# Reordering one of seven Strassen-Winograd products, and the vector work beside it, in the feed-forward stages of a two-layer streaming encoder

## What is computed

```python
def swiglu(h, w_in, w_out):
    gu = h @ w_in
    gate, up = gu[..., :D_FF], gu[..., D_FF:]
    return (jax.nn.silu(gate) * up) @ w_out
# twice per layer: h_res + 0.5 * swiglu(rms_norm(h_res, g), w_in, w_out)
```

## Time and profile before

| | |
|---|---|
| median of 3 runs | 2357.1 us |
| the profiled execution | 2354.26 us |
| its span, first to last instruction | 2352.5 us |
| TensorE matmul busy | 2325.6 us (99%) |
| TensorE weight load busy | 2214.3 us (94%) |
| VectorE busy | 1678.2 us (71%) |
| ScalarE busy | 1242.6 us (53%) |
| granted TensorE clock, mean | 1.0 of full speed |

### The profile page before, as it was taken

The page is one execution under the profiler, slowest core; times in us unless marked ns, Lnnn a source line. Parts: engine busy times, 40 slices in busy tenths (PEclk is TensorE's granted clock), DMA queues, the critical chain, the costliest instruction groups (busy, mean ns, idle before and its releaser), DMA issues.

```text
span 2352.5 us, 43321 instructions
## 1 busy us (share of the span) xinstructions
PE 2325.6 (99%) x17809; PEld 2214.3 (94%) x17809; DVE 1678.2 (71%) x2748; ACT 1242.6 (53%) x2011; POOL 346.3 (15%) x454
## 2 busy tenths in 40 slices
PE   7999999999999999999999999999999999999999
PEld 7999999999999999999999999999888777998997
DVE  8855854899895488568778558548999855874773
ACT  8734733454455477356567347344544455762751
POOL 1101101112212211011011011011222122110110
PEclk9999999999999999999999999999999999999999
DMA  6845736676768968458458457366776698773753
GB/s 179 183 121 144 173 88 154 146 154 149 155 138 199 209 137 182 117 141 187 113 141 182 119 146 168 87 154 149 157 158 150 141 225 190 158 187 102 169 134 110
DMA packets 111365, 358.71 MB, mean 152 GB/s; under 512 B 12608, under 2 KB 12608, under 8 KB 111168
## 3 DMA queue, kind: packets, MB, share of 16 engines
q0 software_dynamic: 64080, 210.53, 44.0%
q1 hardware_dynamic: 46720, 145.08, 21.1%
q10 hardware_dynamic: 368, 0.33, 0.0%
HBM read 351.41 MB, written 2.10 MB: 150 GB/s over the span
## 4 chain that ended last, share of the span: by engine, by line
PE 89%; DVE 5%; ACT 2%; DMA 2%; issue 1%; POOL 0%; DVEq 0%; ACTq 0%
PE po L1102 28%; PE po L1119 23%; PE po L1170 21%; PE ptr L1119 7%; PE pov L1119 5%; DVE cv L1757 1%; DMA wla<-in_mixes 1%; PE pov L1349 1%; PE pov L1352 1%; PE pstat L1309 1%; DMA wha<-in_mixes 1%; PE ptr L1318 1%; PE pov L1289 0%; PE pstat L1274 0%; DVE wlb L1518 0%
## 5 line engine op out<-in xcount | busy, mean ns | idle before, releaser
L1102 PE MATMUL po<-xh,wha 128*128 128x264 f32 (+1 forms) x1408 | 345.5, 312 | 2.7 <-DMA wla<-in_mixes 2.0
L1102 PE MATMUL po<-xl,wha 128*128 128x264 f32 (+1 forms) x1408 | 335.5, 305 | 0.0
L1102 PE MATMUL po<-xh,wla 128*128 128x264 f32 (+1 forms) x1408 | 334.8, 304 | 0.0
L1757 DVE SCALAR_TENSOR_TENSOR cv<-ub,lp,cv 128x528 f32<-128x528 f32 (+1 forms) x480 | 333.3, 753 | 1.7
L1170 PE MATMUL po<-hh,wla 128*128 128x264 f32 (+1 forms) x1232 | 283.7, 300 | 0.0
L1170 PE MATMUL po<-hl,wha 128*128 128x264 f32 (+1 forms) x1232 | 283.7, 300 | 0.0
L1170 PE MATMUL po<-hh,wha 128*128 128x264 f32 (+1 forms) x1232 | 282.6, 299 | 0.4 <-DVE wla L1526 0.4
L675 ACT ACTIVATE wla<-wha 128x1024 fp32r<-128x1024 f32 x136 | 143.8, 1059 | 222.2 <-DMA wha<-in_mixes 222.1
L1526 DVE TENSOR_TENSOR wla<-wfa,wha 128x768 fp32r<-128x768 f32 (+1 forms) x128 | 113.8, 890 | 202.0 <-ACT wha L713 201.9
L1102 PEld LDWEIGHTS po<-xh,wha 128*128 128x128 f32 x1408 | 226.8, 188 | 22.1 <-issue 3.8
L713 ACT ACTIVATE wha<-wfa 128x768 fp32r<-128x768 f32 (+1 forms) x128 | 101.0, 789 | 265.7 <-DMA wfa<-in_outs 265.7
(11 more groups left out here) (240 smaller groups left out, 5676.4 us busy)
## 6 DMA issues: line engine op xcount, KB each, us to landing
wha<-in_mixes POOLq DMA_DIRECT2D x136, 512.0 KB, 4.3
wla<-in_mixes POOLq DMA_DIRECT2D x136, 512.0 KB, 6.4
raw<-in_pairs SPq DMA_DIRECT2D x88, 768.0 KB, 5.6
wfa<-in_outs SPq DMA_DIRECT2D x64, 384.0 KB, 3.1
wlb<-in_pairs POOLq DMA_DIRECT2D x47, 512.0 KB, 8.3
raw<-in_pairs SPq DMA_DIRECT2D x88, 256.0 KB, 6.9
wla<-in_pairs POOLq DMA_DIRECT2D x87, 256.0 KB, 6.6
wfa<-in_outs SPq DMA_DIRECT2D x64, 320.0 KB, 2.9
```

The source lines that it names most:

```text
L1102: ins = mm(po[:, 2 * out_slot + h, 0:width], w[:, k, :], v[:, k, t:t + width], start=begin and k == 0 and p == 0, stop=last and k == kt - ...
L1757: stt(cv[:, j, a:], u, w, cv[:, j, a:], ALU.mult, ALU.add).then_inc(conv_step, 1)
```

## The change

On TensorE, P3(j) is issued ahead of P4(j-1) in place of behind it, in the emitted order and in the numbering. On VectorE, in the general pairs (all but the first two of a stage), `inner(j-1)` comes behind `gate_sum(j,1)` and `gate_norm(j,1)` in place of ahead of them, just ahead of `inner_lo(j-1)`. At a chunk's last pair, `out_lo(s, c, 1)` therefore comes ahead of both. ScalarE's order, the loads and all arithmetic are as they were.

```diff
@@ tensor_order
                 yield "P6", j
+                yield "P3", j
                 if j > s * KF + a:
                     yield "P4", j - 1
-                yield "P3", j
@@ TensorE, ffn
                         seventh("P6", j, X, begin=False, before=x7(3) if opening else None)
-                        if j > j0:
-                            last_product(j - 1)
                         pe.wait_ge(s_lo, 2 * j + 2)
                         pe.wait_ge(e5_done, j + 1)
                         seventh("P3", j, Z, begin=False)
+                        if j > j0:
+                            last_product(j - 1)
@@ VectorE, ffn
                         else:
                             out_lo(s, c, 0)
-                        if j > j0:
-                            inner(j - 1)
                         if j + 1 == j1:
                             out_lo(s, c, 1)
                         gate_sum(j, 1)
                         gate_norm(j, 1)
                         if j > j0:
+                            inner(j - 1)
                             inner_lo(j - 1)
```

## The result

The changed kernel takes 2428.3 us, the median of 4 runs from 2421.7 to 2432.8; the kernel before takes 2357.4 beside it. The ratio is 1.029, with a 95% interval of 1.028 to 1.031. I had forecast 2409 us with a range of 2386 to 2424. The direction and the chain of waits hold. The loss is 71 us where I had 52, and the time lies above the range.

What follows compares the result with a forecast made beforehand. TensorE, 99% busy, sets the pair, but P3's wait for ScalarE's copy_e5 has least slack; 37.6 + 5.6 + 2.5 + 6.4 = 52 us on 2354.3 gives 2406, plus 2.8 for the median, 2409 us; range 2386 to 2424.

Steps and rivals of the forecast that it cites:

- the chain of waits: Regular pairs: later P4 delays ScalarE, then VectorE's sum12, then copy_e5, stalling P3 0.67 us; forecast case, chance 0.76.
- P4 later, `base22_hi` later, `inner_hi` queued behind it: Regular pairs, ScalarE: base22_hi starts 0.26 us after the next pair's P1 starts, inner_hi 1.46; sum12 comes 1.11 later.
- The block back to P3: ScalarE's 3.66 us without idle shifts 1.11; copy_e5 ends 7.85 after P1's start, P3 starts at 8.00, stalling 0.67.
- my 0.88: Last stage's regular pairs: P3 stalls 0.88 us in each of 13, since pairs there are 0.38 shorter.
- VectorE's order at nothing in regular pairs: Regular pairs, VectorE: inner behind gate sum and norm costs nothing, covered by ScalarE not being ready for inner_hi.
- `base_hi` in its own pair is needed for a stall: Only pairs with base_hi in their own pair and the regular order one pair earlier stall: 13 a stage.
- Chunk ends: Before each chunk's output products TensorE waits 0.80 us for inner, eight times, 6.4 us; out_lo(1) moved ahead costs nothing.
- my 0.80 for P4's end: At a chunk's end inner starts 1.47 us later behind P4(9), so the output products start 0.80 late.
- Pair 2: Pair 2 of each stage: P4(1) no longer runs during P3's wait for the copy; 1.4 us, four times, 5.6.
- My forecast's own range: 2396 to 2421 us: stall between 0.5 and 0.85 in 52 pairs, small terms between half and one and a half.
- The rule of the Trainium skill: Judging by occupancy, it picks TensorE to optimise first; so read, reordering equal work beside it is free, sum near nothing.

Runs made afterwards that it cites:

- the first experiment: The changed kernel with VectorE back in its old order, inner ahead of gate sum and norm; 2426.9 us, ratio 1.029.
- both ScalarE edits: The changed kernel with inner_hi(j-1) ahead of base22_hi(j+1), and copy_e5(j) between the two copies of base_hi(j+2); 2406.8 us, ratio 1.021.

## Why the prediction missed, step by step

- **P4 later, `base22_hi` later, `inner_hi` queued behind it**: right, T+0.26 and T+1.46 in the rows, and shown by the experiment that unqueues `inner_hi`.
- **The block back to P3**: right, T+7.85 and T+7.99, shown by moving the copy. The step missed 0.06 a pair, the restart after a stop, 3 us in sum. The other 2.2 of the 5.2 are late loads in two pairs (1.3) and the last stage, where a pair loses 0.96 in place of my 0.88 (0.9).
- **VectorE's order at nothing in regular pairs**: right inside the change, and the experiment with it alone shows that this holds only under the larger wait.
- **"`base_hi` in its own pair is needed for a stall"**: wrong. `up2` is a second release of the same copy, late by the same 1.1 us. It cost 2.3 us.
- **Chunk ends, "`out_lo(1)`, moved ahead, fills a VectorE that idles for 3.11 there, cost nothing"**: this is the step whose reasoning failed, and the largest miss for its size: 11.1 us in place of 6.4. The idle was there, but the moved step itself waits for a load, and a queue in order makes everything behind it wait too. The kernel before had that load landed in time, by T+8.10. With `inner` ahead of the moved step (the first experiment) the eight ends cost 5.9, so my 0.80 for P4's end alone was right.
- **Pair 2**: the 1.4 was right (pair 46: 12.53 against 11.06). In the first experiment's kernel, where no fall touches these pairs, the four cost 5.2 together. The other 3.8 of the 9.0 is the clock, which I had put at nothing without a word. One more fall lies in the mixer part, which with the output products adds 3.0; what else is in these 3.0 stays open.
- **The range**: every term that I left out was a cost, and my upper end stood only 15 us over the sum. My forecast's own range of 2396 to 2421 was also added up too narrow: its stated bounds give 2390 to 2423. The measured 2428 is above that too.
- **The rule of the Trainium skill** (Perfetto Trace Analysis, Identifying the Most-Contended Engine) named TensorE, which is the fullest engine in the trace (94% by its weight loads). By my reading of it the reorder would have been free; it cost 71 us. The page itself says nothing of reorders. The engines with 53% and 71% decided here: in the changed kernel their chain holds TensorE to a pair of 10.99, and with both ScalarE edits they close a loop of 10.6 of their own. What worked is the same page's Optimization Strategy: find the gaps on that engine and what releases them. Here that was `copy_e5`, 59 waits.

## What to carry to other kernels

On an engine at 99%, look for the wait with the least slack and ask what stands in the queues between its release and the step you move: here 1.90 us of slack bore a move of 1.46, but not the 1.11 that the move added through another engine's queue. Add up the loop that the other engines form without the full one, work and idle; when it passes the full engine's period, expect that as the new period, as with the 10.6 us here. And before a step is moved ahead into idle time, look at what that step itself waits for.

## What the runs showed of the hardware

In the profile of the changed kernel the granted clock fell inside the work, in that of the kernel before only at its end. By their mean clock, other executions of the kernel before had falls too: beside the experiments, those with a mean clock of 1.000 took 2355.4 to 2361.0 us, those with 0.998 took 2358.6 to 2364.8. Windows of the kernel after: one fall, then pair 24 with it and pair 46 without:

```profile
887.12:890.53 3.41, 3.41 (x18) 3.41 (x17) 2.09 (x3) 0.66 (x2) 0.31 (x1) 0.50 0.95 265
...
877.20:891.20 14.00, 12.16 (x86) 11.88 (x85) 11.47 (x19) 10.14 (x14) 2.61 (x3) 0.88 0.78 195
1250.36:1262.90 12.54, 10.70 (x87) 10.37 (x86) 11.41 (x19) 10.14 (x14) 2.63 (x3) 1.00 0.77 198
```

A clock of 0.50 is the 1.2 GHz level. In both pairs TensorE had been idle for 1.84 us just before P3:

```profile
886.69 0.36 PE L1119 MATMUL po<-x7h,whb 128*128 128x264 f32 x1 [1.84 <-ACT tmp L726]
```

```profile
1259.87 0.36 PE L1119 MATMUL po<-x7h,whb 128*128 128x264 f32 x1 [1.84 <-ACT tmp L726]
```

The same stop was followed by a fall in one and not in the other; the fall cost 1.47 us. In the first experiment's kernel none of the four pairs 2 has one. The changed kernel's profile has four such falls inside the work, three of them in pairs 2, and those of the experiments have one to six, mostly behind the stops of pairs 2 and of chunk ends. The runs of the changed kernel stand in the order of their mean clock: 0.998 at 2421.7 us, 0.997 at 2425.5, 0.996 at 2431.2 and 2432.8. The profiled one has its 0.997 with four falls inside the work, so a step of 0.001 is one or two falls; at 1.5 us a fall that makes, by my estimate, 3 to 6 of the 11 us. The rest of that spread is not explained, and the 2.7 beside it is of four runs only; 23 runs of the kernel before spread over 8.4. The experiment that gave pairs 2 their old order did not make the falls fewer.
